# The close of a down projection: weights waited for unit by unit, and both splits of a tile ahead of its eviction

## The reference

```
def swiglu(h, w_gu, w_down):
    gate, up = jnp.split(h @ w_gu, 2, axis=-1)
    return (jax.nn.silu(gate) * up) @ w_down
...
h = rmsnorm(x, norm_pre[l, 0])
x = x + 0.5 * rmsnorm(swiglu(h, ffn1_gu[l], ffn1_down[l]), norm_post[l, 0])
```

## Time and profile before

| | us |
|---|---|
| median of 3 runs | 3034.51 |
| lowest, highest | 3028.71, 3036.26 |
| the profiled execution | 3037.89 |
| its span, first to last instruction | 3036.1 |

### The profile page before, as it was taken

How to read it: one execution, slowest core, us unless ns; L and a number is a source line. 1 busy time by engine, 2 the same in 40 slices (tenths; PEclk the granted TensorE clock), 3 DMA queues, 4 the chain that set the end, 5 groups by cost and what they waited for, 6 DMA issues and landing times.

```text
span 3036.1 us, 47084 instructions
## 1 busy us (share of the span) xinstructions
PE 2940.6 (97%) x20842; PEld 2769.6 (91%) x20842; DVE 1311.6 (43%) x1839; ACT 974.6 (32%) x1373; POOL 101.0 (3%) x98
## 2 busy tenths in 40 slices
PE   8999999999999999999999999999999989999997
PEld 7999999995888889999999999899859968999996
DVE  5444226734463364442354432456345535444322
ACT  4222214325444242222232221332354343322211
POOL 0000000000100100000000000000101001000000
PEclk9999999998999999999999999999899999999998
DMA  3222222220242122222222222122203311222321
GB/s 108 81 83 85 87 65 71 63 89 22 74 128 91 49 63 83 79 86 86 69 70 83 83 87 83 54 77 63 89 0 119 112 62 56 77 83 83 89 83 54
DMA packets 420865, 233.03 MB, mean 77 GB/s; under 512 B 7092, under 2 KB 415704, under 8 KB 420728
## 3 DMA queue, kind: packets, MB, share of 16 engines
q1 hardware_dynamic: 414544, 210.33, 23.8%
q0 software_dynamic: 5952, 20.59, 1.9%
q10 hardware_dynamic: 232, 0.08, 0.0%
HBM read 219.44 MB, written 11.54 MB: 76 GB/s over the span
## 4 chain that ended last, share of the span: by engine, by line
PE 88%; DVE 6%; ACT 4%; DMA 1%; issue 0%; ACTq 0%; POOL 0%; DVEq 0%; POOLq 0%
PE PS L340 70%; PE PS L327 3%; PE PS L314 2%; PE PS L610 1%; PE PS L796 1%; DVE w_lo L1171 1%; PE PS L745 1%; PE PS L632 1%; DVE y L1210 1%; PE PS L494 1%; PE PS L657 1%; DVE x L1219 1%; PE PS L357 1%; ACT w_hi L836 1%; DVE h_lo L1179 1%; PE PS L635 1%
## 5 line engine op out<-in xcount | busy, mean ns | idle before, releaser
L340 PE MATMUL PS<-h_hi,w_hi 128*128 128x288 f32 x3712 | 798.9, 297 | 2.0 <-ACT mvT L1103 1.0
L340 PE MATMUL PS<-h_lo,w_hi 128*128 128x288 f32 x3712 | 795.0, 296 | 0.0
L340 PE MATMUL PS<-h_hi,w_lo 128*128 128x288 f32 x3712 | 794.6, 296 | 0.0
L1171 DVE TENSOR_TENSOR w_lo<-raw,w_hi 128x1024 fp32r<-128x1024 f32 (+1 forms) x372 | 491.9, 1322 | 670.3 <-ACT w_hi L836 668.7
L836 ACT ACTIVATE w_hi<-raw 128x1024 fp32r<-128x1024 f32 (+1 forms) x372 | 414.0, 1113 | 659.4 <-DMA raw<-in_ffn_gu_dram 291.8
L340 PEld LDWEIGHTS PS<-h_hi,w_hi 128*128 128x128 f32 x3712 | 597.4, 189 | 5.2 <-issue 1.4
L340 PEld LDWEIGHTS PS<-h_lo,w_hi 128*128 128x128 f32 x3712 | 598.2, 189 | 0.0
L340 PEld LDWEIGHTS PS<-h_hi,w_lo 128*128 128x128 f32 x3712 | 598.2, 189 | 0.0
L340 PE MATMUL PS<-a_hi,w_lo 128*128 128x288 f32 x1232 | 264.0, 296 | 0.0
L340 PE MATMUL PS<-a_hi,w_hi 128*128 128x288 f32 x1232 | 263.9, 296 | 0.0
L340 PE MATMUL PS<-a_lo,w_hi 128*128 128x288 f32 x1232 | 263.7, 296 | 0.0
(11 more groups left out here) (300 smaller groups left out, 3553.6 us busy)
## 6 DMA issues: line engine op xcount, KB each, us to landing
raw<-in_ffn_gu_dram SPq DMA_DIRECT2D x176, 512.0 KB, 3.8
raw<-in_ffn_down_dram SPq DMA_DIRECT2D x64, 704.0 KB, 4.6
raw<-in_w_in_dram SPq DMA_DIRECT2D x52, 512.0 KB, 3.9
raw<-in_w_out_dram SPq DMA_DIRECT2D x16, 512.0 KB, 4.1
raw<-in_w_mk_dram SPq DMA_DIRECT2D x16, 512.0 KB, 4.1
raw<-in_w_mv_dram SPq DMA_DIRECT2D x16, 512.0 KB, 4.1
raw<-in_w_mq_dram SPq DMA_DIRECT2D x16, 512.0 KB, 4.1
raw<-in_w_mo_dram SPq DMA_DIRECT2D x16, 512.0 KB, 4.1
```

What stands on the lines that cost most here:

```text
L340: m = mm(PL[slot][:, h, 0:HT], wt(ws)(a, k), (hi, lo)[b][:, k0 + k, HALF[h]], start=(first and n == 0), stop=(last and n == 3 * kt - 1))
L1171: TT(wlo(c % NW, w_), rawu(c % NW, w_), f32(whi(c % NW, w_)), ALU.subtract).then_inc(wlo_r, 1)
```

## The change

There are two edits, and neither adds or removes an instruction. In TensorE's `close` the wait for all units' splits at the top becomes a wait for each unit's split just before that unit's first matmul of the first half. In ScalarE's and VectorE's `ffn` the second of a tile's two splits, unit b+2m+3, is moved from behind the tile's eviction to ahead of the wait for it.

```
             def close(pn, units, hi, lo, kt):
 
-                for u, _ in units:
-                    pe.wait_ge(wlo_r, u + 1)
                 for h in range(2):
                     for s, (u, k0) in enumerate(units):
+                        if h == 0:
+                            pe.wait_ge(wlo_r, u + 1)
                         for k in range(kt):
...
                 for m in range(KD - 1):
                     upcoming(b + 2 * m + 2)
+                    upcoming(b + 2 * m + 3)
                     act.wait_ge(unit_d, b + 2 * m + 2)
                     post_square(pn, m)
-                    upcoming(b + 2 * m + 3)
                 upcoming(e)
...
                 for m in range(KD - 1):
                     upcoming(b + 2 * m + 2)
+                    upcoming(b + 2 * m + 3)
                     v.wait_ge(unit_d, b + 2 * m + 2)
                     y_tile(pn, m)
-                    upcoming(b + 2 * m + 3)
                 upcoming(e)
```

## The result

The changed kernel took 2996.5 us (median of four runs, 2992.66 to 3003.45) against 3031.61 us for the kernel before (median of four, 3027.66 to 3036.26). The ratio is 0.9886, with a 95% interval of 0.986 to 0.9912: 26.7 to 42.4 us faster, 35 us in the middle.

The account below looks back on a forecast made before the run. TensorE, busy 97%, was taken to bound the kernel, through its idle time and slow matmuls. 15.2 us idle plus 9.75 us clock gave 24.95 us off the 3034.51 us median: 3009.6 us, 8-in-10 range 3002 to 3020.

Parts of the forecast that it names:

- The four waits: At the close of each down projection, TensorE's waits at line 327 for the w_lo split would vanish: 15.2 us.
- the square was not held up by the load: On ScalarE before the close, the load would land at 430.0 us, before unit b+13 ends at 434.05: no delay.
- the next phase's first unit: After the close, its split would be ready by 440.3 us, the half tile at 442.85: 2.5 us or more spare.
- The loss at half clock in the closes: The 78 matmuls behind each of four stalls would return to full rate: 9.75 us, bounds 6.1 to 11.7.
- either edit suffices: At the close, b+15's split would be ready at 437.73 us before 438.45, or at 433.1 before 434.05.
- second price for half clock: At the closes, the Trainium skill's rule, cold duration times 1 - 1.2/2.4, scaled to all four: some 10.2 us.
- with the spread of the runs: Whole kernel: widened 3007.6 to 3013.2 us by 5.8 us below and 1.8 above the median, to 3001.8 to 3015.0.
- the rival that ends slower: Rest of program meets the clock at other instants, mainly mixing, cross-attention, openings; over 0.3% (9.1 us) slower; chance 0.02.
- the forecast was 0.979: Whole kernel: mean granted clock should rise from 0.976 to about 0.979, with 20 us fewer at half rate.
- the clock's loss only moves elsewhere: Openings or other gaps take over the half clock, so only 15.2 us idle time is won: 3019.3 us; chance 0.10.
- nothing is won: Something behind the close keeps its own time and the stall is waited out there: 3034.5 us; chance 0.05.

Follow-up runs that it names:

- first profile of the changed kernel: Profiled execution of the kernel with both edits, in the first measurement against the kernel before: 2994.02 us, 43.9 us less than that of before.
- second comparison: The unchanged changed kernel timed again in five rounds against the kernel before: 3006.64 us against 3031.3, ratio 0.9908 (6 and 17 runs).
- first profile of before: Profiled execution of the kernel without the edits, the one the prediction was read from: 3037.89 us.
- second and third profile: Two more profiled executions of the kernel with both edits, nothing further changed: 3014.19 us and 3000.68 us.

## Why the prediction was right and wrong

**Right: the mechanism, part by part.** The four waits went, all 15.2 us. Nothing took their place: the square was not held up by the load, the next phase's first unit was split by 431.2 us, ahead of the half tile at 433.8, and the next entry of TensorE's waits, 13.0 us, is what it was. The loss at half clock in the closes was put at 9.75 us and measured at 10.2, since the close's own full-rate pace is 10.29 us for 78, not 10.40. That either edit suffices, with 0.7 us to spare for the first alone, was shown at 0.66 us. The closes gave 25.4 us for a forecast of 24.95. (With its second price for half clock, 10.2 us in place of 9.75, the prediction's sum is 25.4 us too, half a us more and not, as it says, less.)

**Wrong: the baseline and its spread.** The step that failed is the one from the sum to the time, "with the spread of the runs (5.8 us below the median, 1.8 above)". It took the median of three runs as the point from which 25 us are taken off, and their spread as all that an execution can differ by. Two terms that differ between executions were not in the sum at all:

- The pace of the first block. I used 0.1333 us per matmul as the full rate; the first block runs at 0.1333 or at 0.1300, and 2940 matmuls make 9.8 us of that. The first profile of the changed kernel had the fast one. By the sorting above, 9.8 of the 13.1 us between the forecast's 3009.6 and the measured 2996.5 are this: the base of 3034.51 us lies in the group with 0.1333 us throughout, and the two times about the median, 2994.02 and 2998.98 us, in the one with a block at 0.1300.
- The half clock in the mixing stretches. The second one took 523.97 and 516.91 us in two executions of the kernel before, 515.91 and 526.31 in two of the changed one. I had this as the rival that ends slower: other instants, other half clock. I weighed it against the three runs' spread alone and let it move the time only upwards; it moves both ways.

Together they can make 17 us between two executions of one kernel, and the ten timed runs of the changed kernel in the two comparisons lie between 2992.66 and 3014.19 us. Four of them made the first median of 2996.5, six the second of 3006.64.

**What remains of the 35 us.** The second comparison's 27.9 us (20.6 to 35.2) contains the 25. At equal pace the change is worth 29 to 30 us, some 4 to 5 more than the closes hold, about twice what the means are uncertain by. The clock points to where it may lie. All ten runs of the changed kernel have a mean granted clock of 0.9821, the 17 runs of before 0.9765; the forecast was 0.979. In half-clock time that is 142.7 - 107.5 = 35 us, which at 0.40 to 0.50 gives 14 to 18 us. The closes hold 10.2 us of it in the first profile of before (8.2 in the second, whose 78s took 12.04, 13.33, 12.07 and 11.96 us), so some 4 to 9 us of clock lie outside the closes, on average over these runs. Whether the change earns them or these runs happened to have them stays open: the kernels without half clock at the closes ranged from 0.9786 to 0.9823 in their means (the one with 13 extra matmuls, and TensorE's half of the change alone).

**The rivals.** That the clock's loss only moves elsewhere, 3019.3 us, is refuted. At equal pace the gain is 29 to 30 us and not 15.2, and the openings did not take the loss over. Those after the first three closes of the changed kernel, in its first profile:

```profile
461.00:471.00 10.00, 9.13 (x48) 8.12 (x49) 5.98 (x13) 4.16 (x9) 0.00 (x0) 0.83 0.18 52
1506.00:1516.00 10.00, 8.47 (x50) 6.88 (x48) 7.16 (x15) 6.01 (x12) 0.00 (x0) 1.00 0.18 54
1942.00:1952.00 10.00, 8.49 (x50) 6.96 (x48) 7.17 (x15) 4.83 (x11) 0.00 (x0) 1.00 0.19 54
```

One of three has a spell at half clock, where the earlier trace rows has two; in the second and third profile none has. That nothing is won, and the slower case, did not happen.

## What to carry to other kernels

A stall of TensorE is priced twice where the clock falls with it: here 3.8 us of waiting cost 1.6 to 3.0 us more in the matmuls behind it, a stall of 1.7 us some 0.3, so read the granted clock behind every wait before you price it. A wait for several things at the top of a stage can be taken apart and put where each is needed; work that is already loaded can go ahead of the wait for something later. And before a forecast takes the median of three runs as its base, ask whether the stages that nobody touches take the same time in two executions; a median of four can be mostly one pace.

## What had not been expected of the hardware

Matmuls of one shape, with a weight load each and the same granted clock of 1.00, keep one of two paces for a whole block of 2940: 0.1300 us or 0.1333 us each. The pace is there from the loop's first units and is kept across every unit's boundary. Of twelve profiles three had the fast one in the first block and one in a later block. TensorE's timeline shows the two, 200 us into the changed kernel's first profile and into its second (rows of two matmuls):

```profile
199.79 0.42 PE L340 MATMUL PS<-h_hi,w_lo 128*128 128x288 f32 x2
200.05 0.42 PE L340 MATMUL PS<-h_lo,w_hi 128*128 128x288 f32 x2
200.31 0.42 PE L340 MATMUL PS<-h_hi,w_hi 128*128 128x288 f32 x2
```

```profile
199.84 0.43 PE L340 MATMUL PS<-h_hi,w_hi 128*128 128x288 f32 x2
200.11 0.42 PE L340 MATMUL PS<-h_hi,w_lo 128*128 128x288 f32 x2
200.37 0.43 PE L340 MATMUL PS<-h_lo,w_hi 128*128 128x288 f32 x2
```

In the first the pairs start 0.26 us apart, in the second 0.27 and 0.26 by turns. The difference is 2.5% of every matmul in the block. Four blocks at the fast pace would save 39 us, more than the change at the closes brought, but no edit here set it.
